# First layer's attention: the second head's half of each projected query and key block copied out of PSUM by VectorE instead of ScalarE

## The chip, the cores and the metric

The kernel runs on one NeuronCore of one Trainium2 chip. Its engines are TensorE (PE in the profile, its weight loads PEld), VectorE (DVE), ScalarE (ACT), GpSimd (POOL) and SyncE (SP, which here only issues DMAs). Each engine runs its own list of instructions in the order in which it was written; engines wait for each other by semaphores. The metric is the time of one execution on the device in microseconds (us), lower is better.

## What is computed

Three transformer-like layers run in one program, over 512 positions of width 1024 in fp32. The change touches the first layer's main attention alone (12 heads, causal, 512 queries and keys):

```python
def mla_mixer(c_q, c_kv, k_r, pos, q_norm, kv_norm, w_q_up, w_kv_up):
    B, S, _ = c_q.shape
    q = (rms_norm(c_q, q_norm) @ w_q_up).reshape(B, S, MLA_HEADS, MLA_QK)
    q_nope, q_rope = q[..., :MLA_NOPE], rope(q[..., MLA_NOPE:], pos)
    kv = (rms_norm(c_kv, kv_norm) @ w_kv_up).reshape(B, S, MLA_HEADS, MLA_NOPE + MLA_V)
    k_nope, v = kv[..., :MLA_NOPE], kv[..., MLA_NOPE:]
    k_rope = jnp.broadcast_to(rope(k_r, pos)[:, :, None, :], (B, S, MLA_HEADS, MLA_ROPE))
    qf = jnp.concatenate([q_nope, q_rope], axis=-1)
    kf = jnp.concatenate([k_nope, k_rope], axis=-1)
    out = causal_block_attention(qf, kf, v, MLA_QK ** -0.5)
    return out.reshape(B, S, MAIN_WIDTH)
```

Beside it run four memory heads over 256 keys. Heads are worked on in pairs. Per head, 64 of the 96 columns of q and k come from a projection of the pair (`q_nope`, `k_nope`), and 32 carry the rotary part.

## The kernel before

**The sweep.** All attention of the layer is one sweep over eight pairs of heads: two memory pairs, then six main pairs. A pair has four steps, one per block of 128 queries. For a main pair the blocks come in the order 3, 0, 2, 1 (line 181), so the steps work on 512, 128, 384 and 256 keys. A step s handles two heads, items 2s and 2s+1.

What each engine does for step s, in the order of its list (`lag` is 2, and DVE has an `early` function):

- PE (`sweep_pe`): scores of step s (L878, and L885 for the causal mask), the transposes of the weights of step s-2 (L896), at the third step of a pair the products with v of the pair before (`values`, L912), and then `turn_in`: some matmuls of the next pair's projections (L1296).
- ACT (`sweep_act`): the exponentials of step s (L952), the copies of the transposed weights of step s-2 back to SBUF (L963, `collect_w`), then `after(s)`.
- DVE (`sweep_dve`): the two negated row maxima of step s+1 (`lowest`, L994), then for each head of step s the reciprocal and the scaling of its weights (`share`, L1000 and L1003), at the third step of a pair the gating of a finished pair (`weigh`, L1011), then `after(s)`.

**The projections.** Product q of the twelve is the query block of pair q/2 where q is even (9 matmuls, 512 wide) and the key block where q is odd (6 matmuls). Its result lies in PSUM bank 0, 128 rows by 512: rows 0 to 63 are the first head of the pair, rows 64 to 127 the second. PE makes the queries of the next pair in a pair's first step (512 keys) and its keys in the third step (384 keys), by `counts` (lines 1333 to 1340).

**The copies out of bank 0.** ACT's `collect(q)` stands in `after(s)` of the same steps, s even. It waits for the product, copies the two halves with one instruction each (L1357, 64 rows by 512, queries scaled), and counts `qk_made` up:

```python
for e in range(2):
    rows = slice(e * HD, (e + 1) * HD)
    ins = nc.scalar.activation((aqT2, akT2)[q % 2][e][p % 2][rows], bank[0][rows, :], ACT.Copy,
                               scale=(QK_A ** -0.5, 1.0)[q % 2])
ins.then_inc(qk_made.sem, 1)
```

Right behind it `split_ahead_act` rounds the weights of product q+2 to their high part (L511), for which POOL then makes the low part (L526); POOL's `copy_rope` (L1155) waits for that and brings the rotary rows of a later pair in place.

PE waits for `qk_made` at two places: before the first matmul of the next product, since bank 0 is one bank (line 1291), and before the first scores of a pair, those on 512 keys (line 1166, the pair's `ready` list: `qk_made` at 2p+2, so both the query and the key block of pair p).

Of the kernel before, what the change touches and what calls it, by code (L numbers as in the profile page):

```python
# [23 lines left out]
ALU = mybir.AluOpType  # L24
# [6 lines left out]
MB = T // P  # L31
# [4 lines left out]
HD = 64  # L36
MEM_H, A_H, B_H = MEM_W // HD, MAIN_W // HD, MAIN_W // HD
NOPE, ROPE = 64, 32
QK_A = NOPE + ROPE
# [181 lines left out]
def build(nc, i, out):  # L221
    ctx = ExitStack()
    with ctx:
# [3 lines left out]
        def count(name):  # L227
            return Count(ctx.enter_context(nc.semaphore(name)))

        bank = [ctx.enter_context(nc.psum_tensor(f"bank{n}", [P, 512], F32)) for n in range(8)]  # L230
# [901 lines left out]

        MP = MEM_H // 2
        qk_made, rope_made, rows_in = count("qk_made"), count("rope_made"), count("rows_in")
        rope_act, rope_copied = count("rope_act"), count("rope_copied")

        def rope_rows(e):
# [23 lines left out]
        def mla_pair(p):  # L1161

            rope_in = (rope_made.sem, 2) if p == 0 else (rope_act.sem, 2) if p == 1 else (rope_copied.sem, 2 * p - 2)
            return Pair(MB, True, lambda e: aqT2[e][p % 2], lambda e: akT2[e][p % 2],
                        lambda c, e: a_v[p // 3][:, c, (2 * p % 6 + e) * HD:(2 * p % 6 + e + 1) * HD], p,
                        ((qk_made.sem, 2 * p + 2), rope_in, pA_v.evac(2 * MB)))
        attA = sweep_stage([mem_pair(p, 0) for p in range(MP)] + [mla_pair(p) for p in range(A_H // 2)])

        def turn_block(pe, N, m, banks):
# [97 lines left out]
        def mla_pe(pe):  # L1267
            S = pA_qk
            done = [0]

            def turn_rope(u):
                if u == 0:
                    pe.wait_ge(qk_made.sem, 2)
                    pe.wait_ge(k_roped.sem, 1)
                else:
                    pe.wait_ge(rope_made.sem, u)
                    pe.wait_ge(rope_act.sem, min(u, 2))
                if u == 1:
                    pe.wait_ge(sem["rope_done"], 1)
                for b in range(MB):  # L1280
                    src = a_qr[:, b, (u - 1) * P:u * P] if u else k_rep[:, b, :]
                    mm = nc.tensor.transpose(bank[0][:, b * P:(b + 1) * P], src, ident[:, :])
                mm.then_inc(sem["head_turned"], 1)

            def project_head(q, x):
                p, kk, t = S.piece0 + q, x // 3, x % 3
                last = (QN, KN)[q % 2] - 1
                if x == 0:
                    pe.wait_ge(w_rest.sem, p + 1)
                    if q:  # L1290
                        pe.wait_ge(qk_made.sem, q)
                    if q == 2:
                        pe.wait_ge(rope_made.sem, RG + 1)
                w = (w_hi, w_lo, w_hi)[t][p % 2]
                acts = (acts_hi, acts_hi, acts_lo)[t]
                mm = nc.tensor.matmul(bank[0][:, :], w[:, kk * P:(kk + 1) * P],  # L1296
                                      acts[:, kk + (0, Q_LORA // P)[q % 2], :], start=x == 0, stop=x == last)
                if x == last:
                    mm.then_inc(C["product"].sem, 1)

            def v_unit(u):

                c, g = u // MB, u % MB
                if g == 0:
                    pe.wait_ge(w_rest.sem, pA_v.piece0 + c + 1)
                if u >= 2:
                    pe.wait_ge(*pA_v.evac(u))
                wh, wl = (w[:, 0:2 * AV].rearrange("p (k n) -> p k n", k=2) for w in w_at(pA_v.piece0 + c))
                for x in range(6):
                    kk, t = x // 3, x % 3  # L1310
                    mm = nc.tensor.matmul(bank[v_bank(u)][:, 0:AV],  # L1311
                                          (acts_hi, acts_hi, acts_lo)[t][:, Q_LORA // P + kk, g * P:(g + 1) * P],
                                          (wh, wl, wh)[t][:, kk, :], start=x == 0, stop=x == 5)
                mm.then_inc(v_made.sem, 1)

            def beside(s):
                if s in V_STEPS:
                    v_unit(2 + V_STEPS.index(s))

            def turn_in(n):  # L1320

                for _ in range(n):
                    x = done[0]
                    done[0] += 1
                    if QKN <= x < QKN + RG + 1:
                        turn_rope(x - QKN)
                        continue
                    if x >= QKN + RG + 1:
                        x -= RG + 1
                    p, x = x // QKN, x % QKN  # L1330
                    project_head(2 * p + (x >= QN), x - QN if x >= QN else x)

            def counts(s):
                if s < 4:
                    return (5, 4, 3, 3)[s]
                if s < 4 * MP:
                    return 1
                if s < 4 * (MP + A_H // 2 - 1):
                    return (QN, 0, KN, 0)[s % 4]
                return 0  # L1340
            v_unit(0)
            v_unit(1)
            pe.wait_ge(*pA_qr.evac(MB))
            sweep_pe(pe, attA, turn_in, counts, beside, lag=2, bank_free=pA_v.evac(2 * MB), begin_next=lambda j: begin_out(pe, pA_out, attA, j))

        def mla_act(act):
            S = pA_qk
            last = 4 * (MP + A_H // 2 - 1)

            def collect(q):  # L1350
                p = q // 2
                act.wait_ge(C["product"].sem, S.done_after(0, q, 0))
                if p >= 2:
                    act.wait_ge(*attA.scored(4 * (MP + p - 1)))
                for e in range(2):
                    rows = slice(e * HD, (e + 1) * HD)
                    ins = nc.scalar.activation((aqT2, akT2)[q % 2][e][p % 2][rows], bank[0][rows, :], ACT.Copy,  # L1357
                                               scale=(QK_A ** -0.5, 1.0)[q % 2])
                ins.then_inc(qk_made.sem, 1)

            def rope_keys():
                act.wait_ge(sem["head_turned"], 1)
                for e in range(2):
                    rows = key_rows(e, 1)
                    ins = nc.scalar.activation(akT2[e][1][rows], bank[0][rows, :], ACT.Copy)
                ins.then_inc(rope_act.sem, 1)

            def rope_queries():
                act.wait_ge(sem["head_turned"], 2)
                act.wait_ge(rope_made.sem, 2)  # L1370
                for e in range(2):
                    rows = rope_rows(e)
                    ins = nc.scalar.activation(aqT2[e][1][rows], bank[0][rows, :], ACT.Copy, scale=QK_A ** -0.5)
                ins.then_inc(rope_act.sem, 1)

            def after(s):
                if s in V_STEPS[4:]:
                    keep_v(2 + V_STEPS.index(s))
                if s < 4 and s % 2:
                    collect(s // 2)  # L1380
                    split_ahead_act(act, S, 0, s // 2)
                if s == 4:
                    rope_keys()
                if s == 5:
                    rope_queries()
                if 4 * MP <= s < last and s % 2 == 0:
                    q = 2 * (s // 4 - MP) + 2 + s % 4 // 2
                    collect(q)
                    split_ahead_act(act, S, 0, q)
                for c in {1: (0, 1), 2: (2,), 3: (3,)}.get(s - last, ()):  # L1390
                    gated_high(act, attA, c)

            def keep_v(u):
                to, of = store_v(u)
                act.wait_ge(v_made.sem, u + 1)
                nc.scalar.activation(to, of, ACT.Copy).then_inc(pA_v.evac.sem, 1)
            keep_v(0)
            keep_v(1)
            sweep_act(act, attA, lambda s: None, after, lag=2)
            for c in range(4, len(attA.pairs)):  # L1400
                gated_high(act, attA, c)

        def mla_dve(dve):
            last = 4 * (MP + A_H // 2 - 1)

            def early(s):
# [6 lines left out]
                if 0 <= u < RG + 1:  # L1413
# [8 lines left out]
                                                      QK_A ** -0.5, None, ALU.mult)  # L1422
                    ins.then_inc(rope_made.sem, 1)

            def after(s):
                if s == last:
                    dve.wait_ge(C["product"].sem, pA_qk.done_after(0, pA_qk.n - 1, 0))
                if s == last:
                    rest_dve(dve, pA_out.piece0 + 1)
                if s == last + 1:  # L1430
                    gated_low(dve, attA, 0)
                    gated_low(dve, attA, 1)
# [1095 lines left out]
```

## Time and profile before

| | |
|---|---|
| time, median of 3 runs | 1189.39 us (1189.06 to 1189.64) |
| time of the profiled execution | 1190.11 us |
| its span, first to last instruction | 1188.4 us |
| PE matmul busy | 1166.4 us, 98% |
| DVE busy | 541.3 us, 46% |
| ACT busy | 604.2 us, 51% |
| POOL busy | 432.0 us, 36% |
| stretch of the sweep that the change touches | about 160 to 250 us |
| copies of L1357 (ACT) | 24 of 0.59 us each |

The profiled execution took 0.72 us more than the median, and 1.71 us of it lie outside the span. The shares of busy time are averages over all three layers. What the change does is decided inside the sweep, where PE, ACT and DVE hand work to each other several times in a step; there the order of time on each engine has to be read, with what it waited for (in brackets behind a row: how long the engine was idle before it, and who released it). A row that stands for several instructions (x2, x4) gives the time from the first one's start to the last one's end.

### The profile page before, as it was taken

The numbers are of one execution on the slowest core, as the hardware profiler recorded it, in microseconds if no ns is written. First come the engines' busy times: TensorE is split into PE (matmuls) and PEld (weight loads), VectorE is DVE, ScalarE is ACT, GpSimd is POOL, SyncE is SP. The second block draws the span as 40 slices with busy tenths as digits, with TensorE's granted clock in tenths as the row PEclk, the third lists the DMA queues.
The fourth block names the chain that finished last, engine by engine and source line by source line (L and its number), as shares of the span: only waits on it lengthen the run. The fifth ranks groups of instructions, "written<-read, shape, count | busy, mean of one in ns | idle before, by whom it ended". The sixth has DMA issues, their size and how long they took to land.

```text
span 1188.4 us, 16087 instructions
## 1 busy us (share of the span) xinstructions
PE 1166.4 (98%) x6031; PEld 917.1 (77%) x6031; DVE 541.3 (46%) x987; ACT 604.2 (51%) x1266; POOL 432.0 (36%) x267
## 2 busy tenths in 40 slices
PE   8999999899999999999999999999999999999998
PEld 7988866578988666668888987887666677888886
DVE  5311475645110655454467556512777750033333
ACT  7444677755353655565545653634655553243242
POOL 6534721134244222214353332444222223444451
PEclk9999999999999999999999999999999999999999
DMA  8533211113335322212332312233222113232321
GB/s 300 144 106 69 65 23 47 54 58 87 99 97 141 91 72 71 72 37 74 106 89 56 123 54 71 84 87 101 67 54 54 54 54 89 88 106 90 104 91 71
DMA packets 111572, 100.98 MB, mean 85 GB/s; under 512 B 21168, under 2 KB 98300, under 8 KB 111496
## 3 DMA queue, kind: packets, MB, share of 16 engines
q1 hardware_dynamic: 108952, 95.38, 27.6%
q0 software_dynamic: 864, 3.15, 0.7%
q10 hardware_dynamic: 1680, 1.44, 0.5%
q8 instruction: 48, 0.79, 0.3%
q14 instruction: 28, 0.23, 0.1%
HBM read 97.83 MB, written 2.12 MB: 84 GB/s over the span
## 4 chain that ended last, share of the span: by engine, by line
PE 91%; DVE 3%; ACT 3%; issue 2%; POOL 1%; DMA 0%; DVEq 0%; ACTq 0%
PE bank L607 50%; PE bank L2019 8%; PE bank L1712 7%; PE bank L1504 6%; PE bank L912 3%; PE bank L878 3%; PE bank L896 2%; PE bank L2035 2%; PE bank L2050 2%; PE bank L2062 2%; PE bank L1296 1%; PE bank L1801 1%; PE bank L717 1%; PE bank L1311 1%; DVE arena L1003 1%
## 5 line engine op out<-in xcount | busy, mean ns | idle before, releaser
L526 POOL TENSOR_TENSOR w_lo<-w_raw,w_hi 128x1024 fp32r<-128x1024 f32 (+4 forms) x157 | 354.5, 2259 | 681.8 <-ACT w_hi L511 681.8
L511 ACT ACTIVATE w_hi<-w_raw 128x1024 fp32r<-128x1024 f32 (+6 forms) x161 | 159.1, 989 | 227.7 <-PE bank L607 203.6
L607 PE MATMUL bank<-acts_hi,w_hi 128*128 128x512 f32 (+1 forms) x576 | 224.0, 389 | 1.0 <-POOL w_lo L526 1.0
L607 PE MATMUL bank<-acts_lo,w_hi 128*128 128x512 f32 (+1 forms) x576 | 222.5, 386 | 0.0
L607 PE MATMUL bank<-acts_hi,w_lo 128*128 128x512 f32 (+1 forms) x576 | 222.5, 386 | 0.0
L607 PEld LDWEIGHTS bank<-acts_hi,w_hi 128*128 128x128 f32 x576 | 108.2, 188 | 24.3 <-POOL w_lo L526 1.5
L607 PEld LDWEIGHTS bank<-acts_lo,w_hi 128*128 128x128 f32 x576 | 108.2, 188 | 22.0
L607 PEld LDWEIGHTS bank<-acts_hi,w_lo 128*128 128x128 f32 x576 | 108.2, 188 | 21.2
L2156 DVE TENSOR_TENSOR_SCAN arena_end<-arena 128x512 f32<-128x512 f32 (+3 forms) x64 | 83.8, 1310 | 59.9 <-ACT arena L2107 59.9
L607 PE MATMUL bank<-w_hi,acts_hi 128*128 128x512 f32 (+4 forms) x240 | 86.9, 362 | 0.2
L607 PE MATMUL bank<-w_hi,acts_lo 128*128 128x512 f32 (+4 forms) x240 | 86.2, 359 | 0.0
L607 PE MATMUL bank<-w_lo,acts_hi 128*128 128x512 f32 (+4 forms) x240 | 86.0, 358 | 0.0
L607 PE MATMUL bank<-w_more,acts_hi 128*128 128x512 f32 (+3 forms) x296 | 75.4, 341 | 0.0
L1003 DVE TENSOR_SCALAR arena<-arena,stat 128x256 f32<-128x256 f32 (+3 forms) x128 | 69.3, 541 | 4.6
L994 DVE TENSOR_REDUCE stat<-bank 128x1 f32<-128x256 f32 (+3 forms) x80 | 33.9, 458 | 77.7 <-PE bank L878 48.5
L2019 PE MATMUL bank<-acts_hi,w_hi 128*128 128x512 f32 x144 | 57.9, 402 | 0.1
L526 POOL TENSOR_TENSOR w_more<-w_raw,w_more 128x1024 fp32r<-128x1024 f32 (+4 forms) x21 | 43.5, 2088 | 39.9 <-ACT w_more L511 39.9
L2019 PE MATMUL bank<-acts_hi,w_lo 128*128 128x512 f32 x144 | 57.5, 399 | 0.0
L2019 PE MATMUL bank<-acts_lo,w_hi 128*128 128x512 f32 x144 | 56.3, 391 | 0.0
L963 ACT ACTIVATE arena<-bank 128x256 f32<-128x256 f32 (+3 forms) x128 | 46.9, 420 | 15.7 <-PE bank L912 14.1
L896 PE MATMUL bank<-ident,arena 128*128 128x128 f32 x304 | 46.8, 279 | 8.0 <-ACT arena L963 7.5
L607 PEld LDWEIGHTS bank<-w_more,acts_hi 128*128 128x128 f32 x296 | 51.5, 188 | 3.8
(307 smaller groups left out, 2125.5 us busy)
## 6 DMA issues: line engine op xcount, KB each, us to landing
w_raw<-in_w_in SPq DMA_DIRECT2D x64, 512.0 KB, 3.7
w_raw<-in_w_out SPq DMA_DIRECT2D x24, 512.0 KB, 3.6
w_raw<-in_w_in_b SPq DMA_DIRECT2D x22, 512.0 KB, 3.9
w_raw<-in_w_in_a SPq DMA_DIRECT2D x10, 512.0 KB, 3.8
w_raw<-in_w_mem_kv SPq DMA_DIRECT2D x8, 512.0 KB, 8.0
w_raw<-in_w_sb_proj SPq DMA_DIRECT2D x8, 512.0 KB, 3.4
w_raw<-in_w_ssd_proj SPq DMA_DIRECT2D x8, 512.0 KB, 3.4
arena_shared<-f_kept_rows SPq DMA_DIRECT2D x11, 256.0 KB, 4.5
```

What stands on the lines that cost most here:

```text
L511: nc.scalar.activation(w_at(p)[0][:, 0:size], w_raw[p % RAW][:, 0:size], ACT.Copy).then_inc(w_high.sem, 1)
L526: nc.gpsimd.tensor_tensor(lo[:, 0:size], w_raw[p % RAW][:, 0:size], hi[:, 0:size].bitcast(F32), ALU.subtract).then_inc(w_rest.sem, 1)
L607: mm = nc.tensor.matmul(bank_of(S, s, g)[0:lhs.shape[1], 0:rhs.shape[1]], lhs, rhs, start=j + kk + t == 0, stop=j == len(S.pieces) - 1 and ...
L878: mm = nc.tensor.matmul(bank[2 + (2 * s + e) % 4][:, 0:n], X.q(e)[:, b * P:(b + 1) * P], X.k(e)[:, 0:n], start=True, stop=not X.causal)
L896: mm = nc.tensor.transpose(bank[6 + i % 2][:, c * P:(c + 1) * P], w2[i % 4][:, c * P:(c + 1) * P], ident[:, :])
L912: mm = nc.tensor.matmul(bank[1][e * HD:(e + 1) * HD, q0:T], X.v(c, e), wT2[e][:, c, q0:T], start=c == 0, stop=c == X.keys - 1)
L963: nc.scalar.activation(wT2[e][:, 0:blocks, b * P:(b + 1) * P], bank[6 + i % 2][:, 0:blocks * P].rearrange("p (c t) -> p c t", c=blocks), A ...
L1003: nc.vector.tensor_scalar(w2[i % 4][:, 0:n], w2[i % 4][:, 0:n], stat[:, 16 + i % 8:17 + i % 8], None, ALU.mult).then_inc(A.weights.sem, 1)
L1504: mm = nc.tensor.matmul(bank[0][:, :], w[:, kk * P:(kk + 1) * P], acts[:, kk, :], start=x == 0, stop=x == 23)
L1712: mm = nc.tensor.matmul(bank[ZB + g][:, 0:n], x_[:, 2 * j + kk, g * P:(g + 1) * P], w[:, kk * n:kk * n + n], start=j + kk + t == 0, stop=j ...
L2019: mm = nc.tensor.matmul(qk_bank(q)[:, :], w[:, kk * P:(kk + 1) * P], acts[:, kk, :], start=x == 0, stop=x == 23)
L2156: nc.vector.tensor_tensor_scan(left[i % 2][:, T - n:T][:, ::-1], x, x, 1.0, ALU.mult, ALU.bypass).then_inc(sem["scan"], 1)
```

## The change

From product 2 on (the second of the six main pairs), ACT's `collect(q)` copies only the first head's half. The second head's half is copied by DVE, in a new `collect_second(q)` that stands in DVE's `after(s)` at the same even steps, with a semaphore of its own, `qk_second`. PE waits for both semaphores at both places. Products 0 and 1 stay as they were.

```diff
+        qk_second = count("qk_second")
+        BY_BOTH = 2
...
             rope_in = (rope_made.sem, 2) if p == 0 else (rope_act.sem, 2) if p == 1 else (rope_copied.sem, 2 * p - 2)
+            second_in = ((qk_second.sem, 2 * p + 2 - BY_BOTH),) if p else ()
...
-                        ((qk_made.sem, 2 * p + 2), rope_in, pA_v.evac(2 * MB)))
+                        ((qk_made.sem, 2 * p + 2), rope_in, pA_v.evac(2 * MB)) + second_in)
...
                     if q:
                         pe.wait_ge(qk_made.sem, q)
+                    if q > BY_BOTH:
+                        pe.wait_ge(qk_second.sem, q - BY_BOTH)
...
+        def head_of_step(s):
+            return 2 * (s // 4 - MP) + 2 + s % 4 // 2
...
-                for e in range(2):
+                for e in range(2 if q < BY_BOTH else 1):
...
+            def collect_second(q):
+
+                p, rows = q // 2, slice(HD, 2 * HD)
+                dve.wait_ge(C["product"].sem, pA_qk.done_after(0, q, 0))
+                if p >= 2:
+                    dve.wait_ge(*attA.scored(4 * (MP + p - 1)))
+                nc.vector.tensor_scalar((aqT2, akT2)[q % 2][1][p % 2][rows], bank[0][rows, :],
+                                        (QK_A ** -0.5, 1.0)[q % 2], None, ALU.mult).then_inc(qk_second.sem, 1)
+
             def after(s):
+                if 4 * MP <= s < last and s % 2 == 0:
+                    collect_second(head_of_step(s))
```

Three places show where the instructions stand. The names: `pair_scores` counts the finished scores of a step, `exped` the exponentials, `valued` the products with v, `product` the projections.

DVE in the third step of a pair, before. The first row is the maxima over 256 keys, then come the weights over 384 keys, the gating, and the maxima over 512 keys of the next pair's first step:

```order
L994 TENSOR_REDUCE stat<-bank 128x1 [waits pair_scores] x2
L1000 RECIPROCAL stat<-stat 128x1 [waits exped]
L1003 TENSOR_SCALAR arena<-arena,stat 128x384 [waits inverse]
L1000 RECIPROCAL stat<-stat 128x1 [waits exped]
L1003 TENSOR_SCALAR arena<-arena,stat 128x384 [waits inverse]
L1011 TENSOR_TENSOR arena<-bank,arena 128x512 [waits valued]
L994 TENSOR_REDUCE stat<-bank 128x1 [waits pair_scores] x2
```

The same place in the changed kernel:

```order
L994 TENSOR_REDUCE stat<-bank 128x1 [waits pair_scores] x2
L1000 RECIPROCAL stat<-stat 128x1 [waits exped]
L1003 TENSOR_SCALAR arena<-arena,stat 128x384 [waits inverse]
L1000 RECIPROCAL stat<-stat 128x1 [waits exped]
L1003 TENSOR_SCALAR arena<-arena,stat 128x384 [waits inverse]
L1011 TENSOR_TENSOR arena<-bank,arena 128x512 [waits valued]
L1439 TENSOR_SCALAR arena<-bank 64x512 [waits pair_scores,product]
L994 TENSOR_REDUCE stat<-bank 128x1 [waits pair_scores] x2
```

The copy of the key block's second half, L1439, stands behind the gating and ahead of the next maxima.

ACT from the first step of a pair into the second, before: the exponentials over 512 keys, two copies of transposed weights, the two copies of the query block, the rounding of weights, and the exponentials over 128 keys:

```order
L952 ACTIVATE arena,stat<-bank,stat 128x512 [waits weights_turned,lowest] x2
L963 ACTIVATE arena<-bank 128x3x128 [waits valued,weights_turned] x2
L1357 ACTIVATE arena<-bank 64x512 [waits pair_scores,product]
L1357 ACTIVATE arena<-bank 64x512
L511 ACTIVATE w_hi<-w_raw 128x384 [waits w_parts2,w_in2,product]
L952 ACTIVATE arena,stat<-bank,stat 128x128 [waits weights_turned,lowest] x2
```

And now:

```order
L952 ACTIVATE arena,stat<-bank,stat 128x512 [waits weights_turned,lowest] x2
L963 ACTIVATE arena<-bank 128x3x128 [waits valued,weights_turned] x2
L1365 ACTIVATE arena<-bank 64x512 [waits pair_scores,product]
L511 ACTIVATE w_hi<-w_raw 128x384 [waits w_parts2,w_in2,product]
L952 ACTIVATE arena,stat<-bank,stat 128x128 [waits weights_turned,lowest] x2
```

One of the two copies is gone; the rest keeps its order.

PE at the first scores of a main pair, in the changed kernel:

```order
L878 MATMUL bank<-arena 128x512 [waits qk_second,evac,exped,rope_copied,qk_made]
```

The wait for `qk_second` has come to those that were there.

## Rows read from the trace of the kernel before

**Rows 1.** The page: busy time of each engine over the whole span.

```profile
PE 1166.4 (98%) x6031; PEld 917.1 (77%) x6031; DVE 541.3 (46%) x987; ACT 604.2 (51%) x1266; POOL 432.0 (36%) x267
```

**Rows 2.** Waits from 160 to 235: waiter, releaser, total us, times, longest.

```profile
ACT arena L952 <- DVE stat L994: 8.1, 5, 1.6
...
PE bank L896 <- ACT arena L963: 4.9, 5, 1.4
```

**Rows 3.** Line 1357: ns min/median/max; who waited for it.

```profile
L1357 ACT ACTIVATE arena<-bank x24: 587/592/592, 143.0 to 232.0; 64x512 f32<-64x512 f32 x24
...
  PEld bank L878: 1.6, 5
```

**Rows 4.** Timeline of PE, one period: start, us, line, operation, count.

```profile
186.32 0.39 PE L1296 MATMUL bank<-acts_lo,w_hi 128*128 128x512 f32 x1
...
187.52 0.39 PE L896 MATMUL bank<-ident,arena 128*128 128x128 f32 x2
187.99 1.98 PE L878 MATMUL bank<-arena 128*128 128x512 f32 x4
189.81 0.28 PE L885 MATMUL bank<-later_keys,ident_b 128*128 128x128 bf16 x2
...
195.29 0.28 PE L885 MATMUL bank<-later_keys,ident_b 128*128 128x128 bf16 x2
196.46 1.06 PE L896 MATMUL bank<-ident,arena 128*128 128x128 f32 x8 [0.90 <-ACT arena L963]
...
202.12 0.28 PE L885 MATMUL bank<-later_keys,ident_b 128*128 128x128 bf16 x2
```

**Rows 5.** Timeline of DVE, the same period.

```profile
187.72 0.76 DVE L994 TENSOR_REDUCE stat<-bank 128x1 f32<-128x256 f32 x2 [5.02 <-PE bank L885]
...
188.58 0.82 DVE L1003 TENSOR_SCALAR arena<-arena,stat 128x384 f32<-128x384 f32 x1
...
190.09 0.68 DVE L1011 TENSOR_TENSOR arena<-bank,arena 128x512 f32<-128x512 f32 x1
190.69 1.27 DVE L994 TENSOR_REDUCE stat<-bank 128x1 f32<-128x512 f32 x2
```

**Rows 6.** Timeline of ACT, the same period.

```profile
186.74 1.19 ACT L1357 ACTIVATE arena<-bank 64x512 f32<-64x512 f32 x2 [0.43 <-PE bank L1296]
...
191.40 0.69 ACT L952 ACTIVATE arena<-bank,stat 128x512 f32<-128x512 f32 x1 [1.64 <-DVE stat L994]
...
193.48 1.19 ACT L1357 ACTIVATE arena<-bank 64x512 f32<-64x512 f32 x2
```

**Rows 7.** Timeline of DVE before the last pair, with POOL idle.

```profile
232.37 0.76 DVE L994 TENSOR_REDUCE stat<-bank 128x1 f32<-128x256 f32 x2 [4.25 <-PE bank L885]
...
233.24 0.42 DVE L1003 TENSOR_SCALAR arena<-arena,stat 128x384 f32<-128x384 f32 x1
...
234.78 1.29 DVE L994 TENSOR_REDUCE stat<-bank 128x1 f32<-128x512 f32 x2
```

**Rows 8.** Timeline of PE before the last pair.

```profile
235.03 0.85 PE L896 MATMUL bank<-ident,arena 128*128 128x128 f32 x6 [0.29 <-ACT arena L963]
```

**Rows 9.** Line 1418, DVE's copies of rotary rows out of bank 0.

```profile
L1418 DVE TENSOR_SCALAR arena<-bank x4: 678/686/695, 151.6 to 155.6; 32x512 f32<-32x512 f32 x2, 64x512 f32<-64x512 f32 x2
```

**Rows 10.** Timeline of POOL, the period of Rows 4.

```profile
188.46 0.73 POOL L526 TENSOR_TENSOR w_lo<-w_raw,w_hi 128x256 fp32r<-128x256 f32 x1 [6.82 <-ACT w_hi L511]
189.34 1.29 POOL L1155 COPY arena<-arena 64x512 f32<-64x512 f32 x2 [0.16 <-POOL w_lo L526]
```

**Rows 11.** Line 705 (filler matmuls), PE: first from 0 to 9.5, then from 9.5 to 14.

```profile
L705 PE MATMUL bank<-tri_le,ident x20: 421/421/582, 4.8 to 9.0; 128*128 128x128 f32 x20
...
L705 PE MATMUL bank<-tri_le,ident x8: 275/275/275, 12.9 to 13.7; 128*128 128x128 f32 x8
```

**Rows 12.** Windows: stretch, us, busy per engine, granted clock, DMA share, GB/s.

```profile
180.00:200.00 20.00, 18.11 (x105) 11.56 (x104) 10.49 (x32) 13.56 (x42) 3.95 (x5) 1.00 0.17 43
```

More of the change, by code:

```diff
@@ L1386, in after @@
                 if 4 * MP <= s < last and s % 2 == 0:
-                    q = 2 * (s // 4 - MP) + 2 + s % 4 // 2
+                    q = head_of_step(s)
                     collect(q)
```

## The prediction

> **What bounds the kernel now.** I read the page's busy shares first: PE is busy 98% of the span, DVE 46%, ACT 51% [rows 1]. So time moves only where PE's waiting changes. Next come the waits of the sweep's stretch. Two rows matter. PE's transposes waited for ACT five times, 4.9 us in all, and ACT's exponentials waited for DVE's maxima five times, 8.1 us in all [rows 2]. The row of line 1357 adds a third: the first scores of a pair waited five times for the copies that the change splits, but only 1.6 us together [rows 3]. These five are the five main pairs after the first.
>
> Then I read the timeline of one period, engine by engine, from the maxima over 256 keys at 187.72 [rows 5] to the next ones, which need the scores whose mask ends at 202.12 + 0.28 = 202.40, so 202.43. A period is 14.71 us, and I cut it in three:
>
> - 187.72 to 187.99: ACT ends the second copy of the key block (186.74 + 1.19 = 187.93) [rows 6], and PE starts the scores on 512 keys at 187.99 [rows 4]. That is 0.27 us.
> - 187.99 to 196.46, 8.47 us: PE's scores, transposes and query projection up to its idle 0.90 us, and then the transposes of the 512 wide weights [rows 4]. They wait for ACT. ACT's list there is exponentials over 512 keys, two copies of weights, **both copies of the query block**, rounding, exponentials over 128 keys, and the copy that frees a PSUM bank. ACT itself began late, at 191.40, after 1.64 us of waiting for the 512 wide maxima [rows 6]. DVE starts these only at 190.69, though their scores ended at 190.09: it was still on the 384 wide weights and the gating [rows 5].
> - 196.46 to 202.43, 5.97 us: PE's own work without a wait that matters.
>
> So ACT and DVE are on the path between PE's pieces, each for a part of the period.
>
> **What is removed.** ACT's L1357 takes 0.59 us [rows 3]; ten of them go, one for each product from 2 to 11. Five are query blocks, on the path of the second part. Five are key blocks, whose end lets PE begin the 512 wide scores.
>
> **What is added.** Ten DVE copies of 64 rows by 512 out of bank 0. The same instruction on the same bank, L1418, takes 0.69 us (two of its four are of the very shape) [rows 9]. I take that row as it is.
>
> **Where the added ones stand.** DVE's list decides.
>
> *Query blocks.* The copy stands behind the weights over 512 keys and ahead of the maxima over 384. DVE waits there 0.50 us for PE in the trace, and its maxima are wanted only by exponentials that wait for PE's transposes anyway. Cost nothing: that wait and the 5.02 us of idle that follow in the third step hide it [rows 5]. Without the cover it would be 0.69 us each.
>
> *Key blocks.* The copy stands behind the maxima over 256, both weight scalings over 384 and the gating, and nothing of these can move. In the trace DVE reaches this slot at 190.69, 2.97 us after 187.72 [rows 5]. The key product has been ready since about 186.71, when the last L1296 ends [rows 4], so neither of the new instruction's waits holds it; DVE's own list does. The copy would end at 2.97 + 0.69, and with 0.06 us to release PE (as 187.93 to 187.99 before) the scores start 3.72 us into the period instead of 0.27. Queued behind this wait on PE are the scores, the transposes of the 384 wide weights and the next query projection; waiting for those scores are DVE's next maxima and through them ACT.
>
> **A correction for POOL.** ACT leaves the key copy 0.59 us sooner, so POOL's L526 and the two rotary copies run that much sooner too. Before, L526 (188.46 + 0.73) lay over the start of DVE's first scaling at 188.58, which took 0.82 us [rows 5, 10]. Before the last pair, with no POOL work there, the same scaling took 0.42, and DVE reached the slot after 234.78 - 232.37 = 2.41 us [rows 7]. Moved forward, L526 ends when the scaling begins, but the rotary copies (1.29 us) still lie over the second one. So the slot is between 2.41 and 2.97; I take 2.75, since one of two overlaps goes. The scores then start at 2.75 + 0.69 + 0.06 = 3.50 (bounds 3.16 and 3.72).
>
> The Trainium skill, SBUF — State Buffer, section "SBUF: two separate sides", says that GpSimd and a VectorE operation in a two-port mode take one pair of ports in turns, whoever starts first holding it for the whole instruction. The trace agrees in kind: 0.82 against 0.42 us [rows 5, 7]. By the full lock the second scaling would wait out a rotary copy of 0.65 us and the slot would come near 2.9, and the sum would be 0.6 us larger; by the rows it is the value above.
>
> **What is given back.** With the scores late, DVE is free when they end. Its 512 wide maxima follow them at once, 190.09 - 187.99 + 0.03 = 2.13 us after their start instead of 2.70, so ACT's chain starts 0.57 us sooner relative to the scores, and it is 0.59 us shorter by the missing query copy. ACT would be ready 1.16 us sooner than the 8.47 us, at 7.31. PE itself is at the end of its 384 wide scores 195.57 - 187.99 = 7.58 us after its start [rows 4]; taken with the release, 7.60. The later of the two decides: the second part shrinks from 8.47 to 7.60, 0.87 us. The third part stays 5.97 us of PE work.
>
> **Sum.** A middle period becomes 3.50 + 7.60 + 5.97 = 17.07 instead of 14.71, so +2.36 us. There are four periods that begin with a key copy and end at another pair: 4 x 2.36 = 9.4. The fifth, before the last pair, has its slot at 2.41, so its scores come at 3.16, +2.89 us; of it the 0.29 us by which the transposes waited for ACT there are given back [rows 8], leaving +2.6. Ahead of the first key copy one query copy is shorter with nothing late: -0.6. Together +11.4 us. After the sweep PE never waits for anything that ran ahead meanwhile, so the delay goes straight to the end. The profiled execution, 1190.11, would be at 1201.5; against the median, 0.72 us lower, it is 1200.8.
>
> **Bounds.** Lowest slot, 3.16: 4 x 2.02 + 2.6 - 0.6 = 10.1, so 1199.5. Highest slot, 3.72, and none of the give-back: 4 x 3.45 + 2.9 = 16.7, so 1206.1.
>
> **The rivals.**
>
> *The clock falls (10%).* PE would stand idle from about 187.91 (the end of L896 [rows 4]) to 191.2, over 3 us, in each of five pairs. Now the granted clock is 1.00 there [rows 12], that is the 2.4 GHz level, and PE's longest idle of the sweep is 1.4 us [rows 2]. Nothing in the sweep shows a longer one. The nearest row is the start: after 4.8 us in which PE had done nothing, twenty matmuls of L705 took 421 ns each (starts from 4.8 to 9.0, so 0.22 us apart), where eight of the same shape took 275 ns later (0.11 us apart) [rows 11]. If some 4.2 us after each stall ran like that, half of it would be lost, 2.1 us a pair: 11.4 + 10.5 = 21.9, so 1211.3. Against it: the idle is a third shorter than the start's, and PE worked without pause up to it. The Trainium skill, TensorE: Matmul & The Clock Gate, Part 1, has the clock fall to its lower level when the engine has been idle for a while and rise again after sustained work; if these stalls count as that, the sum would be this rival's.
>
> *Not slower (3%).* The mechanism would be that DVE has the key half copied by the time PE asks. Then the key side costs nothing, and each of five query copies gives 0.59: -3.0, so 1186.4. It decides at 0.87 us: the copy may delay the scores by that much before the give-back is used up, so it would have to end by 1.1 us into the period, when the two maxima over 256 keys alone take 0.76 [rows 5]. The list puts four operations more in between, so only a misreading of the order would bring it.
>
> *Nothing changes (3%).* ACT's idle before its exponentials (1.64 us [rows 6]) shows slack, and if the wait for DVE were as short as the one for ACT, both edits would vanish in it: 1189.4. For this the third step's DVE work would have to lie elsewhere than in Rows 5.
>
> *Only a size is off* (a give-back that ACT or POOL spoils, a longer copy): inside the bounds above, and part of the forecast.
>
> **How the numbers follow.** The forecast with its bounds has 84%, the clock 10%, the two others 3% each. The range from 1198 to 1206 holds the forecast and its bounds and leaves the clock and the two small ones out. A measurement of this kernel can tell about 0.2%, 2.4 us, from no change. So slower 0.94, within 0.03, faster 0.03.
>
> **What would show it.** In the changed kernel: L1439 of the key blocks starting some 2.4 to 3 us after the maxima over 256 keys; PE idle 3.2 to 3.5 us five times before the 512 wide scores, released by DVE's L1439; the 0.90 us before the wide transposes gone; a period of about 17.1 us; L994 over 512 keys starting at once when the scores end; granted clock 1.00. It is wrong if those five waits are under 1 us, if the wide transposes still wait for ACT, or if matmuls behind the stall are 1.5 times as long as before.

## The result and the profile after

| | before | changed |
|---|---|---|
| time, median | 1189.39 us (5 runs, 1189.05 to 1189.64) | 1211.94 us (5 runs, 1207.28 to 1213.25) |
| ratio | | 1.018 (95% interval 1.017 to 1.020) |
| span of the profiled execution | 1188.4 us | 1205.5 us |
| mean granted clock of TensorE | 1.00 | 0.990 to 0.995 in the five runs |

The change made the kernel 22.6 us slower. The forecast was 1200.8 us with a range from 1198 to 1206, so the sign was right and the size was not: the time is where the rival "the clock falls" had been put, 1211.3 us, with a chance of 10%. The runs of the kernel before lie within 0.6 us of each other, those of the changed one within 6 us. The profiled execution of the changed kernel is its fastest, 1207.28 us.

The stall is where the prediction had put it. This is PE's timeline of the changed kernel around the second of the five key copies (start, us, what; in brackets the idle before and the releaser), to hold against [rows 4]:

```profile
188.58 0.27 PE L885 MATMUL bank<-later_keys,ident_b 128*128 128x128 bf16 x2
188.69 0.39 PE L896 MATMUL bank<-ident,arena 128*128 128x128 f32 x2
192.86 2.39 PE L878 MATMUL bank<-arena 128*128 128x512 f32 x4 [3.78 <-DVE arena L1439]
195.04 0.42 PE L885 MATMUL bank<-later_keys,ident_b 128*128 128x128 bf16 x2
195.25 1.48 PE L896 MATMUL bank<-ident,arena 128*128 128x128 f32 x6
196.39 0.77 PE L1301 MATMUL bank<-acts_hi,w_hi 128*128 128x512 f32 x1
196.96 0.63 PE L1301 MATMUL bank<-acts_hi,w_lo 128*128 128x512 f32 x1
197.39 0.52 PE L1301 MATMUL bank<-acts_lo,w_hi 128*128 128x512 f32 x1
197.75 0.40 PE L1301 MATMUL bank<-acts_hi,w_hi 128*128 128x512 f32 x1
```

PE stands idle 3.78 us for L1439, DVE's copy. Behind the stall its work is slow. The six transposes take 1.48 us; in the kernel before, in the period of [rows 4], they take 0.84:

```profile
189.92 0.84 PE L896 MATMUL bank<-ident,arena 128*128 128x128 f32 x6
```

The matmuls of L1301 shrink from 0.77 to 0.40 us, and only there are they as short as before (0.39 in [rows 4]).

DVE in the same period, to hold against [rows 5]:

```profile
188.89 0.76 DVE L994 TENSOR_REDUCE stat<-bank 128x1 f32<-128x256 f32 x2 [3.05 <-PE bank L885]
...
189.75 0.84 DVE L1003 TENSOR_SCALAR arena<-arena,stat 128x384 f32<-128x384 f32 x1
...
190.70 0.58 DVE L1003 TENSOR_SCALAR arena<-arena,stat 128x384 f32<-128x384 f32 x1
191.20 0.68 DVE L1011 TENSOR_TENSOR arena<-bank,arena 128x512 f32<-128x512 f32 x1
191.91 0.69 DVE L1439 TENSOR_SCALAR arena<-bank 64x512 f32<-64x512 f32 x1
195.50 1.29 DVE L994 TENSOR_REDUCE stat<-bank 128x1 f32<-128x512 f32 x2 [2.89 <-PE bank L885]
```

The copy stands behind the two maxima and five more operations (two reciprocals, two scalings, the gating) and starts 3.02 us after the maxima. DVE itself is then idle for 2.89 us, because its next maxima need the scores that its copy has held up.

The windows of the changed kernel show the clock (columns as in [rows 12], the last three being granted clock, DMA share and GB/s):

```profile
175.70:181.30 5.60, 5.60 (x31) 4.18 (x32) 2.38 (x8) 2.79 (x8) 0.00 (x0) 1.00 0.02 4
...
192.80:198.00 5.20, 5.14 (x17) 3.47 (x18) 2.14 (x6) 1.78 (x6) 0.00 (x0) 0.67 0.00 0
...
192.80:194.00 1.20, 1.14 (x3) 0.68 (x4) 0.00 (x0) 0.00 (x0) 0.00 (x0) 1.00 0.00 0
195.00:196.00 1.00, 1.00 (x7) 0.96 (x6) 0.50 (x1) 0.00 (x0) 0.00 (x0) 0.50 0.00 0
```

The first row stands behind the first stall, the second behind the second. Both stalls were 3.8 us long; behind the first the clock stayed at its upper level of 2.4 GHz (1.00), behind the second it was at the lower one, 1.2 GHz, for a part of the window, which gives the mean of 0.67. The last two rows take that window apart: here the clock did not fall during the stall but more than a microsecond after PE had begun to work again. In this execution it fell after three of five stalls. The executions with a mean clock of 0.990 took 1213 us, the one with 0.995 took 1207.

### The profile page after: what moved, and what is told of

It reads as the page before. It is cut to its first block, busy times and chain, and to the rows that moved or that the text cites. A ratio compares the mean times of both kernels' runs of the same rounds, so it can differ in the third digit from the quotient of the medians.

```text
span 1205.5 us, 16095 instructions
## 1 busy us (share of the span) xinstructions
PE 1170.1 (97%) x6031; PEld 919.5 (76%) x6031; DVE 549.1 (46%) x997; ACT 596.7 (50%) x1256; POOL 432.1 (36%) x267
## 4 chain that ended last, share of the span: by engine, by line
PE 92%; DVE 3%; ACT 2%; DMA 1%; issue 1%; POOL 1%; SPq 0%; DVEq 0%; ACTq 0%
PE bank L607 49%; PE bank L2038 8%; PE bank L1731 7%; PE bank L1523 6%; PE bank L878 4%; PE bank L896 3%; PE bank L912 3%; PE bank L2054 2%; PE bank L1301 2%; PE bank L2069 2%; PE bank L2081 2%; PE bank L1820 1%; DVE arena L1003 1%; DMA w_raw<-in_w_mem_kv 1%; PE bank L717 1%
## 5 line engine op out<-in xcount | busy, mean ns | idle before, releaser
L526 POOL TENSOR_TENSOR w_lo<-w_raw,w_hi 128x1024 fp32r<-128x1024 f32 (+4 forms) x157 | 354.7, 2260 | 699.3 <-ACT w_hi L511 699.3
L2175 DVE TENSOR_TENSOR_SCAN arena_end<-arena 128x512 f32<-128x512 f32 (+3 forms) x64 | 79.5, 1241 | 60.0 <-ACT arena L2126 60.0
L1003 DVE TENSOR_SCALAR arena<-arena,stat 128x256 f32<-128x256 f32 (+3 forms) x128 | 72.5, 567 | 4.6
L878 PE MATMUL bank<-arena 128*128 128x512 f32 (+7 forms) x192 | 52.2, 473 | 18.3 <-DVE arena L1439 18.3
L952 ACT ACTIVATE arena<-bank,stat 128x256 f32<-128x256 f32 (+3 forms) x80 | 39.8, 503 | 46.4 <-DVE stat L994 46.3
L526 POOL TENSOR_TENSOR w_more<-w_raw,w_more 128x1024 fp32r<-128x1024 f32 (+4 forms) x21 | 43.5, 2089 | 40.4 <-ACT w_more L511 40.3
```

What stands on the lines that cost most here:

```text
L526: nc.gpsimd.tensor_tensor(lo[:, 0:size], w_raw[p % RAW][:, 0:size], hi[:, 0:size].bitcast(F32), ALU.subtract).then_inc(w_rest.sem, 1)
L878: mm = nc.tensor.matmul(bank[2 + (2 * s + e) % 4][:, 0:n], X.q(e)[:, b * P:(b + 1) * P], X.k(e)[:, 0:n], start=True, stop=not X.causal)
L952: nc.scalar.activation(w2[i % 4][:, 0:n], src[:, 0:n], ACT.Exp, bias=stat[:, i % 8:i % 8 + 1], scale=-1.0 if X.less else 1.0, accum_out=st ...
L1003: nc.vector.tensor_scalar(w2[i % 4][:, 0:n], w2[i % 4][:, 0:n], stat[:, 16 + i % 8:17 + i % 8], None, ALU.mult).then_inc(A.weights.sem, 1)
L2175: nc.vector.tensor_tensor_scan(left[i % 2][:, T - n:T][:, ::-1], x, x, 1.0, ALU.mult, ALU.bypass).then_inc(sem["scan"], 1)
```

## The experiments

The main theory, called A, is that the place of the key copy in DVE's list makes five stalls of PE, and that some of these stalls bring the clock down; stall and fall each have their own price. The rival, B, is that copies on DVE cost wherever they stand (contention for bank 0, a full DVE, a second semaphore). A third reading leaves the stalls as they are but puts the excess over 1201 us down to something other than the clock.

### Queries alone, keys alone

```diff
-                if 4 * MP <= s < last and s % 2 == 0:
+                if 4 * MP <= s < last and s % 4 == 0:
                     collect_second(head_of_step(s))
```

This is DVE's side of the first kernel; ACT copies both halves where q is odd, and PE's waits count accordingly. The second kernel has `s % 4 == 2` and the reverse on ACT.

> Only the five query copies are shared with VectorE; both halves of every key block stay on ScalarE. Theory A (the loss comes from the place of the key copy in VectorE's list): no late scores, ScalarE's part of each period 0.59 us shorter, five times: 1189.4 - 3.0 = 1186.4 us, granted clock 1.00. Theory B (VectorE's copies cost by themselves, wherever they stand): half of the changed kernel's loss, about 1200 us.

> Only the five key copies are shared; ScalarE copies both halves of every query block. Theory A: the five waits of TensorE before the 512 wide scores are all there (3.2 to 3.8 us), and with ScalarE's 0.59 us back in the second part less is given back, 0.57 us instead of 0.87: some 1.5 us above the changed kernel's 1201 without falls of the clock, so 1203, and 1208 to 1215 with the falls that it had. Theory B: about 1200 us.

Queries alone: **1185.46 us** (1185.15 to 1185.64), ratio 0.9966 (0.9954 to 0.9979), clock 0.999 to 1.000; that is 0.9 us better than A had it. Keys alone: **1214.48 us** (1212.64 to 1215.16), ratio 1.021 (1.019 to 1.023), clock 0.988 to 0.991, as A had it for falls of the clock. So B falls: half of the copies gain, the other half lose at least as much as all together. The loss belongs to the keys and the gain to the queries. In the keys-alone kernel four of five stalls were followed by long scores; the 512 wide scores, 1.98 us in [rows 4], in its timeline of PE:

```profile
195.74 3.75 PE L878 MATMUL bank<-arena 128*128 128x512 f32 x4 [3.77 <-DVE arena L1439]
216.05 3.75 PE L878 MATMUL bank<-arena 128*128 128x512 f32 x4 [3.77 <-DVE arena L1439]
236.43 3.75 PE L878 MATMUL bank<-arena 128*128 128x512 f32 x4 [3.78 <-DVE arena L1439]
256.81 1.95 PE L878 MATMUL bank<-arena 128*128 128x512 f32 x4 [3.20 <-DVE arena L1439]
```

### The stall filled

The changed kernel with matmuls of no use in the stall. They write into the bank that the 512 wide scores overwrite afterwards. Their number, `fill`, was 26, 10, 14 and 4 in four kernels.

```diff
+                if fill and s % 4 == 0 and s > 8:
+                    pe.wait_ge(*A.exped(2 * s - 2))
+                    for _ in range(fill):
+                        nc.tensor.matmul(bank[2 + 2 * s % 4][:, 0:P], ident[:, :], tri_le[:, :], start=True, stop=True)
                 for ready in X.ready if s % 4 == 0 else ():
```

> The changed kernel with 26 idle-time matmuls (128 by 128, about 0.115 us each, 3.0 us in all) put on TensorE in each of the five waits before the 512 wide scores, into the bank that these scores overwrite; nothing else differs and no result depends on them. If what lies above 1201 us is the clock: granted clock 1.00 throughout, no scores at half speed, five runs within 1 us of each other at 1201 to 1202.5. If it is something else (contention, another wait): 1207 to 1213 as the changed kernel, with its spread of 6 us.

Measured: **1212.16 us** (1211.96 to 1212.69), clock 0.999. Neither expectation came out as written. The clock stayed up and the spread shrank to 0.7 us, as A says, but the time did not fall. The filling itself was too long:

```profile
190.94 5.97 PE L871 MATMUL bank<-tri_le,ident 128*128 128x128 f32 x52
196.75 1.88 PE L882 MATMUL bank<-arena 128*128 128x512 f32 x4
```

An fp32 matmul leaves two records, so the 26 show as x52, and one takes 0.23 us, not 0.115. They ran 2.1 us beyond the end of DVE's copy. So this kernel's time says nothing about the excess. The row of L705 in [rows 11] has the same catch: its twenty records are ten matmuls.

> As the filled kernel, but with 10 idle-time matmuls (1.2 us) at the head of each of the five waits, so that TensorE still stands idle for some 2.5 us in one piece. If an idle stretch of that length is short enough for the clock: 1201 to 1202.5, clock 1.00. If it takes the full filling: 1205 to 1213 with a clock under 1.00.

Measured: **1202.68 us** (1202.42 to 1202.87), ratio 1.011 (1.009 to 1.013), clock 0.999 to 1.000. The same stalls, the same copies, the same waits for DVE, and 9.3 us less than the changed kernel, with a spread of 0.5 instead of 6 us. In its timeline of PE, behind the ten matmuls of the second stall, and in its window of the stretch that had 0.67 in the changed kernel:

```profile
192.86 1.95 PE L882 MATMUL bank<-arena 128*128 128x512 f32 x4 [1.55 <-DVE arena L1443]
...
192.80:198.00 5.20, 5.14 (x26) 3.71 (x27) 2.14 (x6) 2.31 (x7) 0.00 (x0) 1.00 0.01 3
```

The scores start at 192.86 in both kernels to the hundredth; only what follows differs, 1.95 against 2.39 us. (This stall was left with 1.55 us of idle in one piece, not the 2.5 us that the expectation had, again because one matmul takes 0.23 us.)

> The changed kernel with 14 idle-time matmuls in each wait: in the first two filled kernels one such fp32 matmul took 0.23 us (two records each), so 14 take 3.2 us and end before VectorE's copy does. If the excess over 1201 is the clock and ten matmuls (1202.7 us) already removed all of it: 1202.7 again within 0.5. If ten left a part of it: below 1202.

Measured: **1202.79 us** (1202.61 to 1202.89), clock 0.999. Filling more changes nothing. So a kernel with the stalls and without the falls takes 1202.7 us, and the rest of the 1211.94 us, 9.3, is the clock.

> The changed kernel with only 4 idle-time matmuls (0.93 us) at the head of each wait; TensorE is then idle for about 3.0 us in one piece instead of 3.8. If the clock falls only behind longer idle stretches: 1202.7 with a spread under 1 us. If any stall of this kind can bring it down: between 1203 and 1212, with a spread of several us and a mean clock under 0.999.

Measured: six runs at 1204.20, 1204.23, 1204.27, 1206.15, 1213.97 and 1215.56 us, with mean clocks of 0.998, 0.998, 0.998, 0.997, 0.990 and 0.988. The second expectation holds for the spread, though the two slowest runs lie above its 1212. The profiled execution is the one of 1204.27 us. Its first four stalls, with 2.89 us idle in one piece, passed without a fall; the fifth, with the shortest stretch, did not:

```profile
227.33 1.95 PE L882 MATMUL bank<-arena 128*128 128x512 f32 x4 [2.89 <-DVE arena L1443]
245.54 3.48 PE L882 MATMUL bank<-arena 128*128 128x512 f32 x4 [2.31 <-DVE arena L1443]
```

So the length of the idle stretch does not decide by itself. From the maxima over 256 keys ahead of the fifth stall to the next ones it is 15.93 us against 14.31 with ten fillers: one fall, 1.6 us, which is about the whole difference between 1204.27 and 1202.68. The other five executions have no trace, and none of them was faster than 1204.20. What decides whether the clock falls, these runs do not show. Two of the six were slower than the kernel without filling; that needs up to 2.6 us for each of five stalls, and the next kernel shows that a fall can cost that much.

### The same stall from ScalarE

The kernel with early key copies (below), where DVE holds nobody up, with ACT's key copy made late:

```diff
+                if q % 2 and q > BY_BOTH:
+                    for n in range(6):
+                        nc.scalar.activation(akT2[0][p % 2][0:HD], bank[0][0:HD, :], ACT.Copy).then_inc(late.sem, 1)
+                        late.total += 1
+                        act.wait_ge(late.sem, late.total)
```

> The kernel with early key copies (1184.6 us), but ScalarE repeats its own half of each key copy six times before it counts it done, so that TensorE waits about 3.7 us before the 512 wide scores for ScalarE, with VectorE's copy long over. If the fall of the clock comes from TensorE's idle stretch, whoever causes it: mean clock 0.990 to 0.996 and 1207 to 1216 with a spread of some us. If it has to do with VectorE's copy or its place: clock 0.999 and a steady time near 1202 to 1204.

Measured: **1207.11 us** (1206.75 to 1208.76), ratio 1.015 (1.014 to 1.016), clock 0.992 to 0.994, at the lower end of what was expected for a fall whoever causes the stall. PE's timeline at three of the five:

```profile
175.41 3.78 PE L878 MATMUL bank<-arena 128*128 128x512 f32 x4 [3.22 <-ACT arena L1371]
195.19 3.57 PE L878 MATMUL bank<-arena 128*128 128x512 f32 x4 [3.22 <-ACT arena L1371]
213.44 1.98 PE L878 MATMUL bank<-arena 128*128 128x512 f32 x4 [3.22 <-ACT arena L1371]
```

The stall was 3.2 us, not 3.7, and the fall comes all the same, with DVE's key copy long over. It is PE's idleness that counts, not who causes it.

This trace also shows that falls differ in price. Its periods are 19.78 us behind the first stall and 18.24 behind the second, both with a fall, and 16.68 behind the third, which had none: 3.1 and 1.6 us for one fall each. PE's windows behind the first and the third:

```profile
175.40:181.00 5.60, 5.59 (x14) 3.24 (x15) 1.52 (x4) 2.32 (x10) 1.95 (x3) 0.50 0.13 28
213.40:218.00 4.60, 4.56 (x21) 3.16 (x22) 2.14 (x6) 3.22 (x12) 1.95 (x3) 1.00 0.31 114
```

Behind the first stall the clock was at the lower level over the whole 5.6 us (0.50), against a part of the window in the changed kernel.

### The key copy elsewhere in DVE's list

First right behind the maxima over 256 keys, ahead of the weights:

```diff
                     lowest(2 * s + 3)
+                if middle:
+                    middle(s)
                 share(2 * s)
```

> The changed kernel, but VectorE copies its half of the key block right behind the maxima over 256 keys, ahead of the two weight scalings and the gating. By theory A the scores start at 0.67 + 0.69 + 0.26 = 1.62 us into a period instead of 0.27, 1.35 us late, of which 0.87 is given back: 4 x 0.48 + 1.06 - 0.6 = +2.4, so 1191.8 us, TensorE's wait at 1.7 us, clock 1.00. By theory B (VectorE's copies cost wherever they stand) 1207 to 1213.

Measured: **1191.97 us** (1191.80 to 1192.15), ratio 1.002 (1.001 to 1.003), clock 0.999. The prediction's arithmetic, with the measured 0.26 us of release and the copy five operations earlier, came out within 0.2 us, but not by its terms: the three middle periods grew by 0.22 to 0.25 us and not by 0.48, and the fourth by 1.3, by a collision that is explained below. PE's stalls were 1.55 us, and ten executions lie within 0.35 us of each other.

Then ahead of the maxima, where DVE was idle:

```diff
             def early(s):
+                if 4 * MP <= s < last and s % 4 == 2:
+                    collect_second(head_of_step(s))
```

> The changed kernel, but VectorE copies its half of the key block before the maxima over 256 keys, where the trace of before has it idle for 5.0 us; the query copies stay where they were put. Theory A: the key copy starts as soon as the product is there and ends before ScalarE's copy used to end, so no wait of TensorE is left and the queries' gain remains: 1185.5 to 1187, clock 1.00. Theory B: as many copies on VectorE as in the changed kernel, so 1207 to 1213.

Measured: **1184.61 us** (1184.41 to 1184.78), ratio 0.996 (0.995 to 0.997), clock 0.999 to 1.000. The best version of the study, 4.7 us below the kernel before and 0.9 below the lower end of what A had expected. DVE's timeline:

```profile
184.93 0.69 DVE L1441 TENSOR_SCALAR arena<-bank 64x512 f32<-64x512 f32 x1 [2.10 <-PE bank L1301]
185.91 0.76 DVE L994 TENSOR_REDUCE stat<-bank 128x1 f32<-128x256 f32 x2 [0.28 <-PE bank L885]
```

The copy begins with the product and ends before the maxima can start; DVE is even idle for 0.28 us between the two. PE's scores follow its transposes without a wait. Ten copies on DVE, as in the changed kernel, and 27 us less.

Last, the query copies moved forward in the same way:

> The kernel with early key copies, and VectorE's query copies moved forward too, ahead of the maxima over 128 keys, where VectorE waits 0.57 us for TensorE. They delay these maxima by 0.1 to 0.2 us and the 512 wide weights with them, and take 0.7 us off the path to the maxima over 384 keys, for which ScalarE waited 1.55 us. If the 384 wide maxima bound a period: 0.3 to 0.5 us less in each of five, 1182.5; if the 512 wide weights do: 0.2 more in each, 1185.5.

Measured: **1184.75 us** (1184.53 to 1184.86), the same as without it. Neither bound named in the expectation was the one that held; a middle period is 13.78 us, and 13.76 without the move.

### The kernel before once more

> The kernel before, unchanged, for a second look at its first 14 us. In its trace VectorE's second pair of 512 wide scalings took 2.51 us over POOL's work and the first projection began at 13.73 us; in the changed kernels' traces it took 1.41 us and began at 12.5 to 13.1. If that collision is chance from run to run, it can be gone here and the span 0.6 to 1 us shorter; if it belongs to this program, it is there again, and the changed kernels gain 0.6 to 1.2 us that the edit does not explain.

Measured: 1189.32 us (1189.24 to 1189.49), span 1187.7 us. The scalings ahead of the first projection, 2.51 us in the first trace of before, took 1.41 us this time, so they differ between executions of the same kernel and are not the edit's doing. This trace begins like those of the changed kernels and is the better one to compare with: its maxima over 256 keys start at 172.36, 187.08, 201.80, 216.50 and 231.75 us. Two of them:

```profile
187.08 0.76 DVE L994 TENSOR_REDUCE stat<-bank 128x1 f32<-128x256 f32 x2 [5.03 <-PE bank L885]
201.80 0.75 DVE L994 TENSOR_REDUCE stat<-bank 128x1 f32<-128x256 f32 x2 [5.02 <-PE bank L885]
```

## Why the prediction was right in its kind and wrong in its size

A period is, as in the prediction, the time from the maxima over 256 keys of one pair to those of the next.

The kernel with ten fillers has the stalls of the changed kernel without the clock, so its periods can be laid beside those of the repeated trace of before.

| | forecast | measured |
|---|---|---|
| ahead of the first key copy | -0.6 | -0.65 |
| three middle periods, each | +2.36 | +2.46, +2.49, +2.52 |
| fourth period | +2.36 | +3.55 |
| last key copy | +2.6 | +2.77 |
| sum, clock up | +11.4 | +13.1 |
| the clock | 0, with a chance of 10% for +10.5 | +9.3 |

**The order and who waits: right.** DVE reached the key copy behind the weights and the gating, PE waited for it five times, and the 0.90 us before the wide transposes were gone. The copy took 0.69 us, as L1418 had [rows 9].

**The slot (2.75 us): a little short.** It was 3.02 us in the middle periods and 2.44 before the last pair. The correction for POOL did not hold. POOL did run earlier, but its first rotary copy then began at 189.78, 0.03 us behind the start of the first scaling, which took 0.84 us as before. Moving POOL's work only changed which part of it lay over DVE's.

**The release (0.06 us): too small.** DVE's copy ended at 191.91 + 0.69 = 192.60 and PE began at 192.86, 0.26 us later. The 0.06 came from the pair ACT and PE, another engine. With both, the scores started 3.97 us into the period and not 3.50.

**The give-back (0.87 us): too small, in the other direction.** The forecast let PE reach the wide transposes 7.60 us after the scores' start. In the changed kernel, behind the first stall, they start at 182.71, 7.03 us after 175.68, since the scores over 128 and 384 keys also come without small pauses. The third part grew by 0.2 us, in which the wide transposes waited for DVE: its second 512 wide scaling took 1.03 us, as it lay under POOL's L526. These errors and the two above nearly cancel, which is why a middle period is off by only 0.1 us; that is luck in the sum.

**The fourth period: a collision not seen.** There ACT rounds a 1024 wide piece, and POOL's work on it came to lie over DVE's 512 wide weights. In the changed kernel DVE shows

```profile
238.71 2.56 DVE L1003 TENSOR_SCALAR arena<-arena,stat 128x512 f32<-128x512 f32 x1
```

and POOL, from 0.06 us before it,

```profile
238.65 2.35 POOL L526 TENSOR_TENSOR w_lo<-w_raw,w_hi 128x1024 fp32r<-128x1024 f32 x1 [9.95 <-ACT w_hi L511]
```

The same scaling for the first head takes 0.49 us, and PE's transposes waited 1.10 us for the long one:

```profile
238.11 0.49 DVE L1003 TENSOR_SCALAR arena<-arena,stat 128x512 f32<-128x512 f32 x1
...
241.33 0.66 PE L896 MATMUL bank<-ident,arena 128*128 128x128 f32 x4 [1.10 <-DVE arena L1003]
```

By the rule of the Trainium skill, SBUF — State Buffer, "SBUF: two separate sides", of GpSimd and a VectorE operation in a two-port mode the one that starts first holds the shared ports and the other waits until it ends. In this trace POOL is ahead and the scaling ended at 241.27, 0.27 us after POOL, which agrees in kind. In the kernel with ten fillers, from which the table's +3.55 comes, the recorded starts are the other way round, and the scaling still took 2.66 us:

```profile
233.85 2.66 DVE L1007 TENSOR_SCALAR arena<-arena,stat 128x512 f32<-128x512 f32 x1
...
233.88 2.35 POOL L526 TENSOR_TENSOR w_lo<-w_raw,w_hi 128x1024 fp32r<-128x1024 f32 x1 [8.39 <-ACT w_hi L511]
```

So starts that the profile shows 0.03 us apart do not tell which of the two waits. The prediction had looked for this sharing in one place only and had taken all four periods as alike. In the trace of before the wide POOL operation lay over 128 wide weights that nobody was waiting for. ACT's shorter list and the late scores together moved it onto wide ones, which are on the path; either alone did not: with keys alone it lay over 128 wide weights again, and with queries alone it began at 220.97, just behind the second wide scaling (220.44 + 0.48).

**The clock: the step that failed.** It was put at nothing in the forecast, and it cost 9.3 us. The sentence was "the clock falls (10%)", with two reasons against it: that the idle would be a third shorter than the one at the start, and that PE would have worked without pause up to it. Neither was a reason that a row bore out. In the trace of before there was no idle stretch of PE between 1.4 us, where the clock held, and 4.8 us, where matmuls were slow afterwards (the granted clock reads 1.00 there too, so only their length speaks for the lower level); 3.3 us lay in the gap between them and the actual 3.8 nearer its far end. A gap without rows is an open question and not one chance in ten. The price was sized well on average: 2.1 us a stall was forecast, and 9.3 / 5 = 1.9 us a stall were lost in the median run, whose number of falls is not known. In the profiled run three falls cost 1.85, 1.35 and 1.56 us (periods of 19.06, 18.57 and 20.36 us against 17.21, 17.22 and 18.80 with fillers), together 4.8, where its time lies 4.6 us above that of the kernel with fillers. That the rival's total, 1211.3, lies within 0.7 us of the median is luck in part: its clock term was 1.2 us too large and its stalls 1.7 us too small. By the Trainium skill, TensorE: Matmul & The Clock Gate, Part 1, a stall of this kind can bring the array's clock down; the traces agree, at 0.67 in the window behind the second stall.

**The range.** It ended at 1206 us and left the clock out as a whole. Since the clock's case stood apart, 5 us above the forecast's own upper bound, its chance alone decided whether the range had to reach it; it rested on the 10%.

**The gain on the queries: under-sized.** The forecast for one ACT copy less was 0.59 us. The queries-alone kernel has periods of 13.81 us instead of 14.72, so 0.91. ACT's timeline there:

```profile
191.67 0.58 ACT L1365 ACTIVATE arena<-bank 64x512 f32<-64x512 f32 x1
192.15 0.52 ACT L511 ACTIVATE w_hi<-w_raw 128x384 fp32r<-128x384 f32 x1
192.56 0.36 ACT L952 ACTIVATE arena<-bank,stat 128x128 f32<-128x128 f32 x1
```

From the start of the copy to the exponentials over 128 keys it is 0.89 us; before it was 195.24 - 193.48 = 1.76. The 0.87 us saved are more than the duration of the copy removed: the distances between the starts of what remains shrank as well, that from the rounding to the exponentials from 0.55 to 0.41 us. Why, the rows do not show. In the changed kernel this gain was covered by PE, whose own work bounded the second part.

## What to carry to other kernels

When work moves to an engine that is idle half of the time, the place in its list decides, not its load: the same ten copies made the kernel 22.6 us slower behind the weights and 4.7 us faster ahead of the maxima, in a gap of 5 us that the trace had shown. Ask of every moved instruction what stands ahead of it on its new engine, and whether the bounding engine waits for its end. If a change makes TensorE stand idle longer than any stretch that the trace shows to be harmless, price the lower clock as a likely case and not as a remote one, and watch for runs that scatter by several us where those of before agree within one. Ten matmuls of no use in each stall are a cheap test that separates the clock from the stall itself.

## What the runs showed of the hardware

- In the eight runs with 10 or 14 fillers, where TensorE was idle for at most 1.55 us in one piece, the mean clock stayed at 0.999 or above; the ten runs with stalls of 1.55 us and no fillers lie within 0.35 us. In the one profiled execution with shorter stretches than 3 us, four of 2.9 us brought no fall and one of 2.3 us did. At 3.2 and 3.8 us some stalls of an execution had one and others did not.
- A fall cost 1.35, 1.6 and 1.85 us in the changed kernel's trace, and 1.6 and 3.1 us in that of the late ACT copy, where the clock stayed at the lower level for longer. It makes the time of a kernel scatter: 6 us here, against 0.6.
- A fall can begin when TensorE is already working again: behind the stall that ended at 192.86 the clock was 1.00 until 194.00 and 0.50 from 195.00 to 196.00.
- VectorE's copy released TensorE 0.26 us after its recorded end, ScalarE's copy after 0.06 us [rows 4, 6].
- A 128 by 128 fp32 matmul, 128 columns wide, leaves two records and takes 0.23 us in a row of such.
